# A linear-attention timetable moved four steps sooner under a dense projection

## What is computed

```
la = log_sigmoid(lr @ w_gate + b_gate) / 16        # "gate logits", then the log of the decay
b  = cumsum(la, within a chunk)
q_in, k_in, k_end = q*exp(b), k*exp(-b), k*exp(b_last - b)
a  = where(lower, q_in @ k_in.T, 0)                # scores, masked by the causal triangle
u  = k_end.T @ v                                   # sums of a chunk
s  = exp(b_last) * s_before + u                    # state, chunk after chunk
o  = a @ v + q_in @ s_before                       # outputs
o  = o * rsqrt(mean(o*o) + eps) * norm_g, times silu(g)
```

## Time and profile before

| what | value |
| --- | --- |
| median of three runs | 3125.92 us |
| the profiled execution's own time | 3126.12 us |
| its span, first to last instruction | 3124.3 us |
| PE / DVE / ACT / POOL busy, share of the span | 95% / 65% / 36% / 23% |
| mean granted TensorE clock | 0.984 of full |

### The profile page before, as it was taken

How to read it: one execution, slowest core, us unless ns; L and a number is a source line. 1 busy time by engine, 2 the same in 40 slices (tenths; PEclk the granted TensorE clock), 3 DMA queues, 4 the chain that set the end, 5 groups by cost and what they waited for, 6 DMA issues and landing times.

```text
span 3124.3 us, 43439 instructions
## 1 busy us (share of the span) xinstructions
PE 2968.1 (95%) x15590; PEld 2526.8 (81%) x15590; DVE 2035.1 (65%) x3370; ACT 1124.8 (36%) x2122; POOL 720.2 (23%) x648
## 2 busy tenths in 40 slices
PE   6999999896899998999999999999999999999997
PEld 4777767674677776878999999999989988888886
DVE  7637745853667766567767567675675748667566
ACT  2247445632334434223434234342332324223221
POOL 0002200002644330132343333433233311000000
PEclk9999999998999999999999999999999999999999
DMA  7889888966977875798898888889889999889874
GB/s 270 318 289 307 269 260 258 283 206 220 282 249 263 253 265 163 256 347 306 285 326 291 297 286 293 302 287 305 265 308 345 350 343 299 258 276 289 263 244 144
DMA packets 481238, 868.40 MB, mean 278 GB/s; under 512 B 40544, under 2 KB 261104, under 8 KB 481024
## 3 DMA queue, kind: packets, MB, share of 16 engines
q1 hardware_dynamic: 353232, 725.08, 69.3%
q10 hardware_dynamic: 111984, 75.97, 8.1%
q0 software_dynamic: 15808, 64.57, 5.7%
HBM read 671.34 MB, written 198.25 MB: 278 GB/s over the span
## 4 chain that ended last, share of the span: by engine, by line
PE 50%; DVE 5%; DMA 3%; issue 1%; ACT 1%; POOL 1%; SPq 0%; ACTq 0%; DVEq 0%; POOLq 0%
PE trunk_ps L76 17%; PE trunk_ps L77 17%; PE trunk_ps L78 16%; DMA shared_ring<-xop 2%; DVE trunk_tt L2582 1%; DVE trunk_tt L2589 1%; DVE trunk_h L2497 0%; DMA shared_spare<-g_s 0%; DMA wop<-trunk_s 0%; PE trunk_ps L2772 0%; DVE trunk_h L2492 0%; POOL trunk_x1t L2152 0%; DVE shared_ring L2539 0%; DVE trunk_h L2479 0%; DVE trunk_stats L2487 0%
## 5 line engine op out<-in xcount | busy, mean ns | idle before, releaser
L76 PE MATMUL trunk_ps<-shared_ring 128*128 128x512 f32 (+2 forms) x1252 | 469.1, 375 | 11.7 <-PEq L1074 5.4
L77 PE MATMUL trunk_ps<-shared_ring 128*128 128x512 f32 (+2 forms) x1252 | 467.3, 373 | 0.0
L78 PE MATMUL trunk_ps<-shared_ring 128*128 128x512 f32 (+2 forms) x1252 | 466.0, 372 | 0.0
L76 PE MATMUL front_acc<-shared_ring 128*128 128x512 f32 x640 | 262.4, 410 | 8.8 <-ACT front_out L580 8.8
L76 PEld LDWEIGHTS trunk_ps<-shared_ring 128*128 128x128 f32 x1252 | 235.6, 188 | 41.3 <-issue 6.9
L78 PEld LDWEIGHTS trunk_ps<-shared_ring 128*128 128x128 f32 x1252 | 236.9, 189 | 27.1
L77 PEld LDWEIGHTS trunk_ps<-shared_ring 128*128 128x128 f32 x1252 | 236.4, 189 | 26.3
L77 PE MATMUL front_acc<-shared_ring 128*128 128x512 f32 x640 | 254.0, 397 | 0.0
L78 PE MATMUL front_acc<-shared_ring 128*128 128x512 f32 x640 | 253.5, 396 | 0.0
L76 PE MATMUL trunk_ps<-shared_ring,trunk_w_more 128*128 128x426 f32 (+1 forms) x648 | 232.8, 359 | 3.6 <-DMA shared_ring<-xop 3.6
L77 PE MATMUL trunk_ps<-shared_ring,trunk_w_more 128*128 128x426 f32 (+1 forms) x648 | 233.3, 360 | 0.0
(11 more groups left out here) (267 smaller groups left out, 6247.9 us busy)
## 6 DMA issues: line engine op xcount, KB each, us to landing
shared_ring<-xt_s SPq DMA_DIRECT2D x280, 512.0 KB, 6.6
shared_ring<-xop SPq DMA_DIRECT2D x312, 426.0 KB, 5.0
shared_ring<-xop SPq DMA_DIRECT2D x168, 428.0 KB, 5.1
shared_spare<-in_w_up SPq DMA_DIRECT2D x198, 256.0 KB, 5.6
shared_ring<-wop SPq DMA_DIRECT2D x46, 512.0 KB, 6.4
wop<-trunk_s ACTq DMA_DIRECT2D x44, 512.0 KB, 5.4
trunk_w_rest<-wop SPq DMA_DIRECT2D x42, 512.0 KB, 6.8
xt_s<-shared_ring SPq DMA_DIRECT2D x40, 512.0 KB, 5.6
```

What stands on the lines that cost most here:

```text
L76: pe.matmul(out, lh, rh, start=first, stop=False, skip_group_check=skip)
L77: pe.matmul(out, lh, rl, start=False, stop=False, skip_group_check=skip)
L78: return pe.matmul(out, ll, rh, start=False, stop=last, skip_group_check=skip)
```

## The change

Three edits. The output steps of all heads and the input steps of heads 2 and 3 are four smaller; heads 0 and 1 keep their input steps. A unit whose input step is also some output unit's mask step gets its logits one step later, and with them its softplus, cumulative sum, exponentials and scaling; the turned keys, sums and copies stay where they were. And `mask` stands first in DVE's step. By the new numbers the later logits fall on the units with input step 105, 109, 113, 117, 121, 125 and 141, which run them at 106, 110, 114, 118, 122, 126 and 142. The list of steps gets four shorter; the dense part still ends with step 159. Distances inside a pass, such as the evictions at steps 111, 119, 127, 135, 143, 151 and 159 and the weight splits at 111 to 118, do not move.

```diff
-IN_AT = {0: [45, 53, 61, 69, 77], 1: [49, 57, 65, 73, 81], 2: [109, 113, 117, 121, 125], 3: [129, 133, 137, 141, 145]}
+IN_AT = {0: [45, 53, 61, 69, 77], 1: [49, 57, 65, 73, 81], 2: [105, 109, 113, 117, 121], 3: [125, 129, 133, 137, 141]}
-OUT_AT = {0: [96, 99, 102, 105, 108], 1: [112, 116, 120, 124, 128], 2: [144, 148, 152, 155, 158],
-          3: [160, 163, 166, 169, 172]}
+OUT_AT = {0: [92, 95, 98, 101, 104], 1: [108, 112, 116, 120, 124], 2: [140, 144, 148, 151, 154],
+          3: [156, 159, 162, 165, 168]}
...
-    logit_at, turn_at, sum_at = in_step, shifted(in_step, 6), shifted(in_step, 8)
-    soft_at, cum_at, exp_at, scale_at, ktok_at, copy_at = (shifted(in_step, k) for k in (1, 2, 3, 4, 7, 9))
     score_at, o_at, back_at = out_step, shifted(out_step, 2), shifted(out_step, 6)
     mask_at, root_at, norm_at, hi_at, lo_at = (shifted(out_step, k) for k in (1, 3, 4, 7, 8))
+    logit_at = [s + 1 if s in mask_at else s for s in in_step]
+    turn_at, sum_at, ktok_at, copy_at = (shifted(in_step, k) for k in (6, 8, 7, 9))
+    soft_at, cum_at, exp_at, scale_at = (shifted(logit_at, k) for k in (1, 2, 3, 4))
...
+                for j in at(mask_at, n):
+                    mask(j)
                 for m in splits_at(n):
                     split(m)
                 for i in at(copy_at, n):
                     copy_sums(i)
                 for i in at(scale_at, n):
                     scale(i)
-                for j in at(mask_at, n):
-                    mask(j)
```

## The result

The changed kernel takes 3134.46 us (median of nine runs, 3133.16 to 3138.71) against 3126.31 of the kernel before beside it (nine runs, 3123.50 to 3128.79): a ratio of 1.0028, 95% interval 1.0020 to 1.0036. It is slower by 8 us where 3 us less were forecast. The time lies in the range; the sign was wrong. The execution that was profiled took 3133.16 us, the shortest of the nine; that of the kernel before took 3126.12.

The account below looks back on a forecast made before the run. TensorE, 95% busy, was taken to lose time only to waits and lower clock (36.8 us in steps 113 to 155). New waits +4.4, head 0 +0.9, tail -8.6 make -3.3: 3123 us, range 3106 to 3136.

Parts of the forecast that it names:

- Score waits behind the later softplus: Scores at 112, 120, 144 wait 7.7, 6.6, 4.7 us for ScalarE's key copy; clock costs 3.4, 3.4, 2.7 more.
- I price these waits at nothing: Logits at 106 to 126 and outputs behind them: masked copies, now first in their step, cause no wait; 0 us.
- Step 142: Logits at 142 still wait for the mask because queued updates hold VectorE; 1.5 us taken.
- the prediction's own signs of being wrong: Softplus at 111 and 119 ending before keys turn, logits waits of 2 us or more, head 0's first outputs waiting over 3.
- The chain to step 133: Five-step chain, 32.8 us, ends in VectorE's low part; sums of 133 wait 6.7, clock 3.2; 1.3 more at 129.
- Head 0's sooner outputs: Updates pressed into steps 84 to 91; the outputs of 94 may wait 0 to 3 us, 0.9 taken.
- Tail: From step 160: three dense parts fill the waits before head 3's first outputs, leaving 1.3 of 9.9 us; -8.6.
- The longer half clock behind the new waits: Rival: four new waits each keep half clock some 8 us more, costing 4 each; +16, 3138 us, chance 0.18.
- The tail did shrink: Judges the rival that head 3's loads wait as before or hold weight loads, so no tail gain; 3131 us, chance 0.10.
- The short chain: Rival: chain to 133 under 26 us, softplus off the critical path there; -13, 3109 us, chance 0.20.
- the case without waits: Rival: all waits vanish, later logits and tail do all they could; -44.5, 3082 us, chance 0.07.
- Table loads: Softplus priced at 1.29 us per load without drain; seven drains of 1.38 would add 9.7, about 3133; under 1 in 50.

Follow-up runs that it names:

- the first experiment: Changed kernel with softplus, cumulative sum, exponentials and scaling back at their old distance from the input step: 3100.75 us, ratio 0.9919 to the kernel before.
- the sixth experiment: Changed kernel with softplus alone back behind the input step; cumulative sum, exponentials and scaling stay one step later: 3121.29 us, ratio 0.9989 to the kernel before.
- the ninth experiment: Changed kernel with VectorE's copies of the chunk sums put ahead of masked copies and splits in their step: 3133.54 us, ratio 1.0023 to the kernel before.
- the tenth experiment: Changed kernel with head 2's 38 backward updates (steps 131 to 139) on 16 columns in place of 128: 3127.34 us, ratio 1.0008 to the kernel before.
- the eighth experiment: The first experiment's kernel with head 3's outputs back at steps 160 to 172: 3099.02 us, ratio 0.9907 to the kernel before.

## Why the prediction was wrong

- **Score waits behind the later softplus: right.** Forecast 7.7, 6.6 and 4.7 us, measured 7.55, 6.49 and 4.69, and the first and sixth experiments show the cause. The clock behind them was put a little high: 3.4, 3.4 and 2.7, measured 1.9, 2.4 and 2.0.
- **"I price these waits at nothing": the step that failed first.** It looked at what stands ahead of the masked copies inside their step. What counts is the step before: the cumulative sum had moved with the softplus and stood right ahead of the masks and the copied sums. Step 118 costs 5.3 us (2.27 and 3.0), and the sixth experiment shows the wait staying when only the softplus goes back. The 3.0 of clock does not follow from the wait each time: in the sixth and the ninth experiment nothing is lost behind it. The outputs also wait for copied sums, not for masks alone, which the step left out.
- **Step 142: right mechanism, wrong size.** 1.5 us were allowed; 4.67 of waiting and 2.8 of clock came, and the 3.46 at the logits is one of the prediction's own signs of being wrong. VectorE did what was forecast: from the cumulative sum (580.14) to the logits behind the mask (625.00) it took 44.9 us, 1.2 less than before (579.80 to 625.84), which is the scaling passed. But TensorE reached the step of the mask 33.7 us behind that cumulative sum (613.81), and not 37.8 (617.63). It no longer stood 0.89 us at 137 and 2.52 for a DMA at 141; the forecast counted these waits and the clock behind them as saved, and did not let TensorE arrive at the full VectorE that much sooner. The 5.2 of before, less 1.2, less 2.8 for the dense part and 1.2 for the chunk sums that now stand ahead of the logits, with these 4.2, make 4.2; measured are 0.60 at the sums of 141 and 3.46 at the logits. This is an estimate from the two traces that no run tried by itself. The 1.21 at the outputs, which wait for copied sums, comes on top. That a full VectorE holds step 142 is shown by the tenth experiment.
- **The chain to step 133: right cause, wrong place.** It was to arrive in one wait of 6.7 with 3.2 of clock. TensorE met it earlier, at the sums of 129 (2.29, behind a normalising) and the turn back of 130 (1.88, behind ScalarE's copied sums), and 133 kept 0.77. Together 8.9 us for 11.2. In the sixth experiment, with the softplus back, the wait at 129 goes, but 2.18 at 130 and 0.80 at 133 stay, for 0.42 and 0.27 in the first experiment; so most of these two belongs to the later step of the cumulative sum.
- **Logits beside sums: left out.** The sum took TensorE's work as unchanged. Five units lost their side-by-side start, 1.9 us, read from the windows and not tried by itself.
- **Head 0's sooner outputs: right**, 0.8 for 0.9 (a wait of 0.57 at step 94).
- **Tail: right in size, and right about the dense parts.** About -8 for -8.6. Head 3's first scores wait 0.66 in place of 3.20, because one dense part more stands in nearly the same time (see the eighth experiment). Its first outputs do not wait for 2.56 any more either, but the outputs of the unit after now wait 2.33, so the waits of this stretch fell by 5.1 in all.
- **Rivals.** The longer half clock behind the new waits did not happen at 112, 120 and 144. The tail did shrink. The short chain and the case without waits are out with the 129 to 133 stretch.
- **Table loads.** In the changed kernel, too, the Ln of step 119's softplus follows the start of its load of 1.28 after 1.30 (515.28 and 516.58). The Trainium skill, "ScalarE: Activation LUTs", section "What ACT_TABLE_LOAD costs", has 1.38 us of draining besides; this trace shows none, and the score waits, short of the forecast by 0.15 at most, leave no room for it.

The terms that were off (5.3 at 118, 6.0 at 142, 1.9 for logits, less 3.5 at the score waits, less 2.3 at the chain) make 7.4 of the 8.5 us between the forecast of -3.3 and the measured +5.2 at the next stage. Small waits that the sum did not have add some 2, the tail adds half a us, and the kernel before lost 37.8 and not 36.8, 1.0 the other way; that closes the sum within half a us. (Of those 36.8, the logits behind masked copies have 27.8 by the prediction's own rows, not about 27; nothing hangs on it.) The other part of the measured 8 us is not explained beyond the spread of the rest of the span. That the time stayed in the range is in part luck: 13.2 us of errors on one side met 5.8 on the other.

A version faster than both kernels is the first experiment, and the eighth beside it (3100.75 and 3099.02, not told apart): the change's idea with one line corrected, the logits one step on and nothing that follows them.

## What to carry to other kernels

When an instruction is moved a step, what follows it moves too: look on each engine at the step into which it falls, and at what stands in the step after. An operation placed behind an eviction on ScalarE and ahead of a copy for which TensorE waits cost its whole length here (7.55 less 2.42, for a softplus of 5.2 with its loads); one placed right ahead of short copies on VectorE cost a part of it (2.27 of 4.7). A wait that is taken away upstream makes an engine arrive sooner at the next full one, and part of it can come back there, as at step 142 by the estimate above. For a wait behind a load, add up the work that the waiting engine has between the instruction that frees the buffer and the one that reads it; a distance in steps says little by itself.

## What the runs showed of the hardware

In step 137 the first matmul of the logits and the first of the chunk sums started 0.01 us apart (601.92 and 601.93), and the two groups together cost 0.38 us less than apart. In the tail the same 230 matmuls took 27.5 to 37.3 us of busy time, from the granted clock alone, with waits that differ by under 3 us; so an experiment whose effect is below some 7 us needs the windows of the tail beside its time.
